# Weights of a hybrid diffusion layer laid out so that a 2 MB transfer reads 16 KB per partition

## What is computed

```
for each layer l:
  shift1, scale1, gate1, shift2, scale2, gate2 = silu(cond) @ w_ada[l] + b_ada[l]   # 1024 x 6144
  h = rmsnorm(x) * (1 + scale1) + shift1
  q, k, v, xr, gr, ga, gb = split(h @ w_in[l])                                      # 1024 x 5632
  att = attention(q, k, v, cached k and v);   rnn = bidirectional gated scan of conv(xr)
  merged = sigmoid(ga) * (att @ w_attn_proj[l]) + sigmoid(gb) * ((gelu(gr) * rnn) @ w_rnn_proj[l])
  x = x + gate1 * (merged @ w_out[l])
  h2 = rmsnorm(x) * (1 + scale2) + shift2
  x = x + gate2 * (top 2 of 16 experts: w_gate_up[l, e] 1024 x 1024, w_down[l, e] 512 x 1024)
final rmsnorm
```

## Time and profile before

| | kernel before |
|---|---|
| median of three runs | 1765.71 us |
| profiled execution, its span | 1765.8 us |
| PE busy | 1626.6 us (92%) |
| PE weight loads | 1075.4 us (61%) |
| DVE busy | 625.9 us (35%) |
| ACT busy | 563.8 us (32%) |
| POOL busy | 135.4 us (8%) |
| q1, SP's queue | 112064 packets, 326.04 MB |
| q0, GpSimd's queue | 11152 packets, 27.80 MB |
| q10, ScalarE's queue | 9024 packets, 22.03 MB |
| HBM over the span | 213 GB/s |

### The profile page before, as it was taken

How to read it: one execution, slowest core, us unless ns; L and a number is a source line. 1 busy time by engine, 2 the same in 40 slices (tenths; PEclk the granted TensorE clock), 3 DMA queues, 4 the chain that set the end, 5 groups by cost and what they waited for, 6 DMA issues and landing times.

```text
span 1765.8 us, 17572 instructions
## 1 busy us (share of the span) xinstructions
PE 1626.6 (92%) x6715; PEld 1075.4 (61%) x6715; DVE 625.9 (35%) x1459; ACT 563.8 (32%) x1021; POOL 135.4 (8%) x214
## 2 busy tenths in 40 slices
PE   4999999999959999999859999998995899999996
PEld 3599866589834444444358987667993444444445
DVE  3347666646440000000042665676555100000002
ACT  1233579932111111111122356995212111111112
POOL 0100022100010000000040001220001000000001
PEclk9799999989969999999979999998997899999998
DMA  9356431236458999998363552212505699999963
GB/s 353 112 207 224 148 103 56 95 104 226 169 201 291 336 333 339 335 337 325 144 218 136 203 190 100 101 60 97 191 1 226 215 338 335 337 334 337 336 219 132
DMA packets 132329, 377.08 MB, mean 214 GB/s; under 512 B 7816, under 2 KB 11280, under 8 KB 132240
## 3 DMA queue, kind: packets, MB, share of 16 engines
q1 hardware_dynamic: 112064, 326.04, 51.9%
q0 software_dynamic: 11152, 27.80, 4.2%
q10 hardware_dynamic: 9024, 22.03, 3.2%
HBM read 351.19 MB, written 24.66 MB: 213 GB/s over the span
## 4 chain that ended last, share of the span: by engine, by line
PE 85%; DVE 6%; ACT 4%; issue 3%; ACTq 1%; POOL 1%; DMA 1%; DVEq 0%; POOLq 0%
PE bank L739 25%; PE bank L471 22%; PE bank L750 12%; PE bank L460 9%; PE bank L481 2%; PE bank L654 2%; PE bank L731 2%; PE bank L830 1%; PE bank L497 1%; PE bank L490 1%; PE bank L627 1%; PE bank L564 1%; PE bank L559 1%; PE bank L785 1%; POOL hT L1760 1%
## 5 line engine op out<-in xcount | busy, mean ns | idle before, releaser
L739 PE MATMUL bank<-ring,ga 128*128 128x512 f32 x768 | 334.9, 592 | 0.0
L1691 DVE SCALAR_TENSOR_TENSOR gr<-gr,bank 128x512 f32<-128x512 f32 x32 | 22.0, 688 | 646.3 <-ACT gr L1144 646.3
L739 PEld LDWEIGHTS bank<-ring,ga 128*128 128x128 f32 x768 | 144.2, 190 | 173.2 <-issue 173.2
L460 PE MATMUL bank<-hT,ring 128*128 128x384 f32 x576 | 197.9, 499 | 19.5 <-POOL hT L1760 12.1
L471 PE MATMUL bank<-parts_r,ga_r 128*128 128x384 f32 x768 | 202.6, 345 | 0.0
L750 PE MATMUL bank<-ring,ga 128*128 128x512 f32 x384 | 168.9, 593 | 3.7 <-issue 3.7
L460 PEld LDWEIGHTS bank<-hT,ring 128*128 128x128 f32 x576 | 109.3, 195 | 91.6 <-issue 21.3
L1144 ACT ACTIVATE gr<-bank 128x512 f32<-128x512 f32 x32 | 19.1, 598 | 396.3 <-PE bank L739 396.3
L471 PEld LDWEIGHTS bank<-parts_r,ga_r 128*128 128x128 f32 x768 | 138.3, 188 | 5.9 <-issue 5.0
L471 PE MATMUL bank<-parts_r,gb_r 128*128 128x384 f32 x384 | 129.7, 338 | 0.0
L750 PEld LDWEIGHTS bank<-ring,ga 128*128 128x128 f32 x384 | 71.2, 190 | 85.4 <-issue 85.4
(11 more groups left out here) (283 smaller groups left out, 2240.1 us busy)
## 6 DMA issues: line engine op xcount, KB each, us to landing
ring<-in_w_gate_up SPq DMA_DIRECT2D x48, 2048.0 KB, 9.8
ring<-in_w_ada SPq DMA_DIRECT2D x24, 2048.0 KB, 8.4
ring<-in_w_down SPq DMA_DIRECT2D x24, 2048.0 KB, 9.0
ring<-in_w_in SPq DMA_DIRECT2D x22, 2048.0 KB, 7.8
parts<-in_w_gate_up SPq DMA_DIRECT2D x16, 2048.0 KB, 9.8
parts<-in_w_down SPq DMA_DIRECT2D x8, 2048.0 KB, 8.9
expert_rows<-gb ACTq DMA_DIRECT2D x32, 512.0 KB, 8.2
ring<-in_w_attn_proj SPq DMA_DIRECT2D x4, 2048.0 KB, 8.3
```

The costliest lines, as they stand in the source:

```text
L460: mm = pe.matmul(bank[:, 0:width], slot_kn(slot)[:, k, n * P:(n + 1) * P], rhs(k), start=(k == 0), stop=(k == KT - 1))
L739: mm = pe.matmul(G[n][0:CAP, :], xt[:, half * 4 + k, 0:CAP], slot_wide(slots[half])[:, k, n * 512:(n + 1) * 512], start=(half == 0 and k = ...
```

## The change

The host lays the seven weight arrays out before the launch, in `laid_out`, so that what a partition receives of a chunk lies in one run of 16 KB, and the 128 runs of a chunk follow one another. The kernel's sources are rewritten for these shapes. What lands in SBUF, at which place, is the same as before, and so are all instructions of the engines, their order and their waits. The host's work is not in the device time.

```diff
-        gu_w = w_gate_up.rearrange("l e (h k p) n -> l e h p k n", p=P, h=2)
-        dn_w = w_down.rearrange("l e (k p) n -> l e p k n", p=P)
+        gu_w = w_gate_up.rearrange("l e h p (k n) -> l e h p k n", k=4)
+        dn_w = w_down.rearrange("l e p (k n) -> l e p k n", k=4)
...
-            return w[l].rearrange("(k p) n -> p k n", p=P)[:, :, c0:c0 + CHUNK]
+            return w[l, c0 // CHUNK].rearrange("p (k n) -> p k n", k=KT)
...
+def laid_out(name, a):
+
+    if name in ("w_ada", "w_in", "w_attn_proj", "w_rnn_proj", "w_out"):
+        n = a.shape[2] // CHUNK
+        return a.reshape(DEPTH, KT, P, n, CHUNK).transpose(0, 3, 2, 1, 4).reshape(DEPTH, n, P, KT * CHUNK)
+    if name == "w_gate_up":
+        return a.reshape(DEPTH, NE, 2, 4, P, 2 * DE).transpose(0, 1, 2, 4, 3, 5).reshape(DEPTH, NE, 2, P, 8 * DE)
+    if name == "w_down":
+        return a.reshape(DEPTH, NE, 4, P, D).transpose(0, 1, 3, 2, 4).reshape(DEPTH, NE, P, 4 * D)
+    return a
...
-        a = np.ascontiguousarray(inputs[name])
+        a = np.ascontiguousarray(laid_out(name, np.asarray(inputs[name])))
```

## The result

The changed kernel takes 1775.7 us in the median of its runs (1772.2 to 1778.1), the kernel before 1766.2 us (1762.9 to 1768.9). The ratio is 1.0056, with a 95% interval of 1.0041 to 1.0071: 0.4 to 0.7% slower. The forecast was 1776.4 us, slower. The profiled execution has a span of 1772.8 us, and its reported time is 1774.94 us. The two differ by 2.1 to 2.3 us in every profiled run here, so the profiled execution of the kernel before, with its span of 1765.8 us, took about 1768 us by this estimate and was one of the longer ones of its kernel.

What follows compares the result with a forecast made beforehand. TensorE, busy 92% of the span, was taken as the bound, with weights early and ScalarE's load queue on the path at the start. A 10.6 us later release gave 1765.8 + 10.6 = 1776.4 us; 8-in-10 range 1761.5 to 1780.

Steps and rivals of the forecast that it cites:

- Nothing in the steady stages: Dense and expert stages: tiles land perhaps 0.5 us sooner, covered by early issue and the 21.9 us cadence; costed at nothing.
- One packet for one, whatever its length: Start, three full DMA queues: each moves one packet a round whatever its size, 0.247 us a round before the change.
- A round costs 0.82 us: Start: a three-queue round with a 16 KB packet costs 0.247 - 0.088 + 0.66 = 0.82 us.
- q10 would be fed better ahead of 10.6 us: Start, lower end: with fewer SP packets to make, q10 moves some 34 an engine by 10.6 us; ScalarE free 8.7 us later.
- ScalarE is let go when its queue has moved 55.8 packets an engine: Start, L899: ScalarE's issue is held until q10 has moved 892/16 = 55.8 packets an engine, at 19.8 us before the change.
- a ring that is full at about 90 packets: Start: each queue has its own ring, full at about 90 packets an engine, read from 90 for q10 and 91 for q1.
- The sum: Whole kernel: ScalarE released 8.7 to 12.6 us later, middle 10.6, added to 1765.8 for 1776.4 us; chance 58%.
- The upper end: Start: 20.2 us of long rounds plus 1.6 us from 10.6 us release ScalarE at 32.4 us, 12.6 us later.
- What gives it back? Nothing on the chain: From L903 to the first projection and after: nothing regains the delay, so the kernel ends 10.6 us later.
- no change at the start: Rival, 20%: runs are cut up or long ones don't hold their turn; 1765.8 us, or 1769 with 4 KB pieces.
- Held longer than forecast: Rival, 8%, start: long packets also slow q0's or are dearer in the mix; above 1780 us.
- Faster through a place that both queues share: Rival, 14%: SP's packets fill a shared place that holds L899; fewer packets free ScalarE 6.6 us sooner, 1759.2 to 1762.8 us.

Runs made afterwards that it cites:

- e1: The changed kernel with w_ada alone back in its old layout, runs of 2 KB; 1765.2 us, ratio 0.9997 to the kernel before.
- e4: The changed kernel with w_ada's tiles still one block of 2 MB each, but in runs of 8 KB; 1774.1 us, ratio 1.0051 to the kernel before.
- e7: The changed kernel with router loads behind ScalarE's first two condition instructions and GpSimd's zero stores waiting for ada2; 1761.7 us, ratio 0.9985 to the kernel before.
- e8: The changed kernel with router_w padded by the host and read as one run of 1 KB a partition; 1760.4 us, ratio 0.9971 to the kernel before.
- e9: The changed kernel with SP issuing weight tile ada1 only once the vector loads have landed; 1767.2 us, ratio 1.0006 to the kernel before.
- e2: The kernel before with w_ada alone in runs of 16 KB; 1773.7 us, ratio 1.0053 to the kernel before.
- e10: The kernel before with router_w read as one run of 1 KB a partition; 1762.9 us, ratio 0.9986 to the kernel before.

## Why the prediction was right

**Nothing in the steady stages**: right. The expert's interval is 21.92 us, tiles land 0.3 us sooner, and e1 shows no gain or loss from the other 130 tiles that its interval of 0.1% either way could tell.

**One packet for one, whatever its length**: right, at four lengths: 596/595/597 in the earlier trace rows, 211/208/208 after, 459/460/459 with 4 KB and 324/319/317 with 8 KB. Even counts can't tell turns of one from turns of nine packets, as was said ahead. The rate of the changed kernel can: it dips about every 0.8 us, the length of one round, so the turns are of one packet.

**A round costs 0.82 us**: too high. Counted with its share of closing packets (0.16 us for a round with one) it was 0.71. From 20 to 24 us q1 of the changed kernel takes 76.6% of 16 engines for 94 packets, of which 80 are long (1.31 MB):

```profile
q1 hardware_dynamic: 94, 1.31, 76.6%
q0 software_dynamic: 94, 0.36, 21.7%
q10 hardware_dynamic: 94, 0.07, 5.5%
```

That is 49.0 us of engine time for the 80, 0.61 us for one, where I had 0.66 from the rates of shorter packets. A 16 KB packet in the round is then 0.247 - 0.088 + 0.61 = 0.77 us. The packets' own times in the traces of before, after and e4 say the same: the medians are 84, 159, 309 and 611 ns for 2, 4, 8 and 16 KB. Eight packets of 2 KB take 0.67 us and one of 16 KB 0.61, and a price taken from the rate of short packets carries that difference into the long one.

**q10 would be fed better ahead of 10.6 us** (the lower bound): wrong. SP's second issue did shrink, from 3.93 to 0.71 us, but q10 had moved 286 packets by 10.6 us, and 295 before. The making of SP's packets isn't what kept it short.

**ScalarE is let go when its queue has moved 55.8 packets an engine**: wrong as a number. It was 46.9. With w_ada in runs of 4 or 8 KB it was 62 to 63; in e7 it was far more, at 36 us:

```profile
q10 hardware_dynamic: 2091, 0.75, 8.2%
```

130.7 an engine, of the 146 that it had been given ahead of L899. So a ring that is full at about 90 packets on the average doesn't hold as a rule. What stands is that the hold is one of the issuing queue's own packets (e8), and that long packets in the other queue stretch it (e1 to e4, e9). A ring on each of the 16 engines, of which the slowest counts, could fit this: in e7 the average is nearly empty while something still isn't. No run shows it, since the profile doesn't list a queue's packets by engine. What ends the hold stays open.

**The sum**: the release was forecast for 28.5 to 32.4 us and came at 29.3, 9.5 us later than before where the middle said 10.6; at the first projection it was 10.06. The upper end had the mechanism's shape and three terms that were too large: the round (24 x 0.05 = 1.2 us), the start of the long packets (13 of them, 0.8 of a round on each engine, were through at 10.6, 0.6 us), and the 55.8 (nine packets at 0.16 us, 1.4 us). Together 3.2 us, and 3.1 were measured. From this upper end I had taken 2 us off for a catch-up that didn't take place. So the middle came out well by luck: a wrong reason to go lower made up for terms that were too large. The base of the sum was lucky too. The 1765.8 us are a span, and the time of that execution was some 2.2 us more; what they were added to as a time is right only because the median of the runs, 1765.7, happens to be the same number.

**"What gives it back? Nothing on the chain"**: right for the chain, but silent on the clock. In the profiled pair some 3 us came back at clock steps, as shown above. That isn't a property of the change. At the start e1 and e2 differ by the longer hold alone, like the two kernels compared, and in their profiles the clock comes back to 1.00 at the same point of the work, 3.4 us into the first projection (at 60.1 and 70.1 us). The chain at the first projection, in e1 and in e2 (that view ends at 74 us and cuts its row short):

```profile
56.72 12.34 PE bank L462 x32
...
66.66 7.54 PE bank L462 x17
```

The delay is 9.94 us there and 9.9 us at the end (spans 1759.9 and 1769.8). And e1 and the kernel before, which release ScalarE at the same time (19.82 and 19.83 us) and whose medians can't be told apart, have spans of 1759.9 and 1765.8 us: the third L481 group of the start takes 1.85 us in one and 3.16 in the other. A single pair of spans is uncertain by several microseconds; the medians say 9.5 us for the change and 8.5 for e2 against e1.

**The rivals**: no change at the start, out (L899 at 16.82). Held longer than forecast, out (released at 29.3). Faster through a place that both queues share, out: SP is no longer held and ScalarE is. SP's first three weight issues in the changed kernel, against the earlier trace rows:

```profile
L423 SPq DMA_DIRECT2D ring<-in_w_ada x3: 432/503/712, 3.7 to 4.9; - x3
```

What this rival said would be late next was right all the same. It put the vector loads at about 38 us and the time at 1759.2 to 1762.8, and once e8 took the hold away, they landed at 38.05 and the time was 1760.4.

## What to carry to other kernels

Before lengthening a transfer's contiguous runs, look for queues that share the DMA engines with it. Where queues take turns by the packet, a long packet takes bytes from every queue that has short ones, and a hold of such a queue falls on the engine that issues into it. The DMA rate rose from 409 to 438 GB/s in the stretch in which ScalarE's queue moved half of its bytes. A load of 64 KB in 1024 runs of 64 B cost 2.4 us in the kernel before and 15.3 in the changed one, by what the two gain with it in 128 runs (e10 and e8). A compute engine that issues loads ahead of its first work should issue few packets, and moving them behind that work only helps if nothing on the chain comes after them on the same engine.

## What was not expected of the hardware

The hold of an issue doesn't end at a fixed average of packets moved: 46.9 to 130.7 an engine over the ten kernels that have one. Runs of 8 KB hold ScalarE as long as runs of 16 KB (16.94 and 16.82 us), while 4 KB add 3.7 us to the 7.12 of 2 KB. And two executions with the same release of ScalarE, those of e1 and of the kernel before, have spans 5.9 us apart, with medians that can't be told apart: the granted clock stepped at other points of the work. In the profiled pair of the comparison this hid 3 of the 10 us.
